# Moving ScalarE and VectorE work inside the second attention of a two-block network: layer-norm silu in two parts, row operands ahead of slab roundings and exponentials

## The reference, cut to what matters

```python
def mixer_ab(h, w_in, conv_w, ln_g, ln_b, w_out):
    u = h @ w_in
    u_val, u_gate, q, k, v = jnp.split(u, ...)
    z = causal_depthwise_conv(u_val * sigmoid(u_gate), conv_w)     # 31 taps, 512 channels
    ya = jax.nn.silu(layernorm(z, ln_g, ln_b))
    yb = moba_attention(q, k, v)                                   # 8 heads of 64, ALiBi, causal at 256 tokens
    return jnp.concatenate([ya, yb], axis=-1) @ w_out
```

## Time and profile before

| what | value |
| --- | --- |
| median of three runs | 894.98 us (894.68 to 895.58) |
| the profiled execution | 894.98 us, span 893.2 us, mean granted clock 0.995 |
| PE busy | 871.1 us, 98% of the span |
| DVE, ACT, POOL busy | 606.9, 470.1, 94.0 us |
| second attention with its projection rows | about 356 to 440 us |
| `mixer_c` up to its projection's end | about 630 to 703 us |

### The profile page before, as it was taken

One profiled execution on the slowest core, in us unless ns is written; L12 is line 12 of the kernel. 1 busy time (PEld: TensorE's weight loads), 2 busy tenths in 40 slices (PEclk: granted clock), 3 DMA queues, 4 the chain that ended last, 5 costly groups with the idle time before them and its releaser, 6 DMA issues.

```text
span 893.2 us, 19362 instructions
## 1 busy us (share of the span) xinstructions
PE 871.1 (98%) x7310; PEld 839.0 (94%) x7310; DVE 606.9 (68%) x994; ACT 470.1 (53%) x755; POOL 94.0 (11%) x139
## 2 busy tenths in 40 slices
PE   8999999999999999997999999999999999999996
PEld 8988899999999999776899999999899999999996
DVE  4766568656656688786766666667979976666665
ACT  6546766434434485356654444445777644444443
POOL 3320002000000039410110000001210100000000
PEclk9999999999999999998999999999999999999999
DMA  7533346565565558422555555555435565555551
GB/s 248 169 120 99 111 138 219 189 207 178 176 203 180 182 167 236 150 96 95 165 189 188 188 188 188 188 189 189 142 123 172 171 204 186 190 189 190 187 180 48
DMA packets 44434, 152.10 MB, mean 170 GB/s; under 512 B 5604, under 2 KB 6884, under 8 KB 44388
## 3 DMA queue, kind: packets, MB, share of 16 engines
q1 hardware_dynamic: 41184, 145.52, 49.7%
q0 software_dynamic: 2400, 4.89, 1.8%
q10 hardware_dynamic: 804, 1.04, 0.3%
HBM read 148.64 MB, written 1.05 MB: 168 GB/s over the span
## 4 chain that ended last, share of the span: by engine, by line
PE 89%; DVE 5%; ACT 4%; issue 1%; DMA 1%; SPq 0%; DVEq 0%; ACTq 0%
PE bank L1342 27%; PE bank L1344 26%; PE bank L1343 26%; DVE alo L938 2%; PE bank L1692 1%; DVE wlo L914 1%; PE bank L1376 1%; PE bank L1426 1%; ACT whi L509 1%; PE bank L1471 1%; DMA raw<-in_slabs 1%; PE bank L1448 1%; PE bank L1370 1%; DVE af L1302 1%; DVE h L948 1%
## 5 line engine op out<-in xcount | busy, mean ns | idle before, releaser
L1342 PE MATMUL bank<-ahi,whi 128*128 128x256 f32 (+1 forms) x1400 | 401.3, 287 | 6.9 <-DVE alo L932 6.1
L1343 PE MATMUL bank<-alo,whi 128*128 128x256 f32 (+1 forms) x1400 | 394.7, 282 | 0.0
L1344 PE MATMUL bank<-ahi,wlo 128*128 128x256 f32 (+1 forms) x1400 | 394.6, 282 | 0.0
L914 DVE TENSOR_TENSOR wlo<-raw,whi 128x1024 fp32r<-128x1024 f32 x273 | 332.7, 1226 | 31.1 <-ACT whi L509 31.0
L509 ACT ACTIVATE whi<-raw 128x1024 fp32r<-128x1024 f32 x273 | 282.7, 1051 | 103.3 <-PE bank L1344 93.4
L1342 PEld LDWEIGHTS bank<-ahi,whi 128*128 128x128 f32 x1400 | 264.8, 189 | 11.1 <-DVE alo L932 6.7
L1343 PEld LDWEIGHTS bank<-alo,whi 128*128 128x128 f32 x1400 | 264.8, 189 | 0.4
L1344 PEld LDWEIGHTS bank<-ahi,wlo 128*128 128x128 f32 x1400 | 265.0, 189 | 0.0
L1342 PE MATMUL bank<-hidhi,whi 128*128 128x256 f32 x704 | 195.0, 277 | 0.5 <-issue 0.5
L1344 PE MATMUL bank<-hidhi,wlo 128*128 128x256 f32 x704 | 195.1, 277 | 0.0
L1343 PE MATMUL bank<-hidlo,whi 128*128 128x256 f32 x704 | 194.4, 276 | 0.0
(11 more groups left out here) (222 smaller groups left out, 721.3 us busy)
## 6 DMA issues: line engine op xcount, KB each, us to landing
raw<-in_slabs SPq DMA_DIRECT2D x273, 512.0 KB, 3.4
shared<-in_convw POOLq DMA_DIRECT2D x4, 512.0 KB, 6.7
shared<-zpad POOLq DMA_DIRECT2D x48, 35.5 KB, 3.5
raw<-in_slabs SPq DMA_DIRECT2D x8, 128.0 KB, 5.6
vtok<-in_gatew POOLq DMA_DIRECT2D x2, 512.0 KB, 4.1
out<-y SPq DMA_DIRECT2D x4, 256.0 KB, 2.7
h<-in_xT ACTq DMA_DIRECT2D x3, 272.0 KB, 5.4
h<-in_xT SPq DMA_DIRECT2D x1, 272.0 KB, 3.6
```

The costliest lines, as they stand in the source:

```text
L914: dve.tensor_tensor(wlo[:, n % R, :, :], raw[:, n % R, :, :], whi[:, n % R, :, :].bitcast(F32), ALU.subtract).then_inc(lo_done, 1)
L1342: pe.matmul(dst, hi, xh, start=start, stop=False, skip_group_check=True)
L1343: pe.matmul(dst, hi, xl, start=False, stop=False, skip_group_check=True)
L1344: return pe.matmul(dst, lo, xh, start=False, stop=stop, skip_group_check=True)
```

## The change

- In the second attention ACT's order changes. In even slots the roundings of slabs (`split_ahead`) come after the transposed probabilities, the pair's output copy and the exponentials; odd slots up to 11 keep theirs in front. Row operands come before the roundings. Operand 0 is made at the end of slot 11 rather than at the start of 12. Output copies go ahead of the exponentials (`PAIR_STEP`), the fourth behind the loop. The exp/tanh table is still loaded in slot 13, but tanh and scaled copy of chunks 0, 1 run in slot 15 and of 2, 3 in slot 17 (were all four in slot 13, ahead of operand 1).
- DVE: the layer norm's product moves from slot 13 to 12, the join of silu follows ACT to slots 15 and 17, slab rests go to the places in `DVE_SPLITS`, the first two final residuals from slot 11 to 18, and behind the loop the three last operands are made ahead of rests and residuals.
- ACT rounds the last three slabs behind operand 7 and around the table load for exp/ln.
- First attention: DVE makes the projection's operand 0 before a slab's rest (`ROW1_SLOT - 1`).
- `mixer_c`: gate products of chunk k run after column k+3, 6 and 7 together after column 9 (were 0 after 3, 1 and 2 after 4, then one each). ACT rounds operand 0 in column 13 rather than 14; DVE's gated output 0 and operand 0 follow `take` of column 13.

```diff
+PAIR_STEP = {6: 0, 10: 1, 14: 2}
+LN_MEAN_STEP, LN_VAR_STEP, LN_NORM_STEP, SILU_STEP = 9, 11, 13, {15: (0, 1), 17: (2, 3)}
-FINAL_RESIDUAL, RESIDUAL_ROW = {11: (0, 1)}, {5: (2, 3), 6: (4, 5), 7: (6, 7)}
+FINAL_RESIDUAL, RESIDUAL_ROW = {18: (0, 1)}, {5: (2, 3), 6: (4, 5), 7: (6, 7)}
+DVE_SPLITS = {13: (-1,), 14: (0, 1), 16: (2,), 17: (3,), 18: (4,)}
-GATES = {3: (0,), 4: (1, 2)} | {k + 2: (k,) for k in range(3, KC)}
+GATES = {k + 3: (k,) for k in range(6)} | {9: (6, 7)}
...
             for u in range(MOBA_U + 3):                      # ACT
-                if u in IN2_STEP or u in OUT2_STEP:
+                slab = u in IN2_STEP or u in OUT2_STEP
+                if slab and u % 2 and u < max(IN2_STEP) + 1:
                     split_ahead(n)
                     n += 1
...
+                    if u in PAIR_STEP:
+                        pair = PAIR_STEP[u]
+                        act.wait_ge(o_ready, FOX_S + 2 * pair + 2)
+                        act.activation(af[:, PAIR_CHUNK[pair], :], aux_bank[:, 0:SEQ], ACT.Copy).then_inc(af_ready, 1)
...
                         probabilities(u // 2, FOX_S, MOBA_N)
+                if u in CAT2_STEP and u > max(IN2_STEP) + 1:
+                    operand_hi(A_CAT2, F_CAT2, CAT2_STEP[u])
+                if slab and (u % 2 == 0 or u > max(IN2_STEP)):
+                    split_ahead(n)
+                    n += 1
...
+                if u == max(IN2_STEP):
+                    act.wait_ge(slab_used, OUT2)
+                    operand_hi(A_CAT2, F_CAT2, 0)
...
                 if u == LN_NORM_STEP:
                     exp_tanh_tables()
-                    for k in range(CONV_C):
+                if u in SILU_STEP:
+                    for k in SILU_STEP[u]:
                         act.wait_ge(ln_norm, k + 1)
...
             for i in range(max(CAT2_STEP.values()) + 1, KC):
+                if i == KC - 1:
+                    act.wait_ge(o_ready, FOX_S + MOBA_S)
+                    act.activation(af[:, PAIR_CHUNK[3], :], aux_bank[:, 0:SEQ], ACT.Copy).then_inc(af_ready, 1)
                 operand_hi(A_CAT2, F_CAT2, i)
-                split_ahead(OUT2 + i)
+            split_ahead(OUT2 + KC - 3)
+            split_ahead(OUT2 + KC - 2)
             exp_ln_tables()
...
+            split_ahead(OUT2 + KC - 1)
             residual_hi(N_MLP0)
...
-                if i == 14:
-                    operand_hi(A_LRU, F_LRU, 0)
                 if i in (13, 14):
                     gelus(3 * (i - 13), 3 * (i - 12))
+                if i == 13:
+                    operand_hi(A_LRU, F_LRU, 0)
...
-                if u == ROW1_SLOT:                           # DVE, first attention
-                    operand_lo(A_MIX1, 0)
...
+                if u == ROW1_SLOT - 1:
+                    operand_lo(A_MIX1, 0)
                 if u >= 1:
                     split_ahead(n)
...
                 softmax_slot(u, MOBA_S, FOX_S, MOBA_N, alibi_bias)   # DVE, second attention
-                if u == LN_NORM_STEP:
+                if u in CAT2_STEP and u > max(IN2_STEP) + 1:
+                    operand_lo(A_CAT2, CAT2_STEP[u])
+                if u == LN_NORM_STEP - 1:
                     dve.wait_ge(ln_std, 1)
...
-                    take(n, acc_bank[n % 2], c, QSCALE if 8 <= c < 12 else 1.0, ahead=n < OUT2 - 1)
+                    take(n, acc_bank[n % 2], c, QSCALE if 8 <= c < 12 else 1.0, ahead=u < 8)
                     n += 1
+                    if u > 8 and n < OUT2:
+                        split_ahead(n - 1)
+                if u == 9:
+                    split_ahead(n - 1)
...
+                if u >= max(IN2_STEP) + 2:
+                    for m in DVE_SPLITS.get(u, ()):
+                        split_ahead(OUT2 + m)
...
             for i in range(max(CAT2_STEP.values()) + 1, KC):
                 operand_lo(A_CAT2, i)
+            for i in range(max(CAT2_STEP.values()) + 1, KC):
                 split_ahead(OUT2 + i)
                 for k in RESIDUAL_ROW[i]:
                     final_residual(k)
...
-                if i >= 14:                                  # DVE, mixer_c
-                    gated_output(i - 14)
-                take(IN3 + i, col_bank(i), c, ahead=IN3 + i < OUT3 - 1 and i not in (10, 14))
-                if i == 14:
+                if i == 15:
+                    gated_output(1)
+                take(IN3 + i, col_bank(i), c, ahead=IN3 + i < OUT3 - 1 and i != 10)
+                if i == 13:
+                    gated_output(0)
                     operand_lo(A_LRU, 0)
-                    split_ahead(IN3 + i)
```

More of the change, by code:

```diff
@@ L118 @@
 OUT2_ORDER = (4, 5, 6, 0, 1, 2, 3, 7)
-LN_MEAN_STEP, LN_VAR_STEP, LN_NORM_STEP, SILU_STEP = 9, 11, 13, 15
+PAIR_STEP = {6: 0, 10: 1, 14: 2}
+LN_MEAN_STEP, LN_VAR_STEP, LN_NORM_STEP, SILU_STEP = 9, 11, 13, {15: (0, 1), 17: (2, 3)}
 PLAIN_COLUMN = 4
-FINAL_RESIDUAL, RESIDUAL_ROW = {11: (0, 1)}, {5: (2, 3), 6: (4, 5), 7: (6, 7)}
+FINAL_RESIDUAL, RESIDUAL_ROW = {18: (0, 1)}, {5: (2, 3), 6: (4, 5), 7: (6, 7)}
+DVE_SPLITS = {13: (-1,), 14: (0, 1), 16: (2,), 17: (3,), 18: (4,)}
 SQUARES_ROWS, SQUARES_CHUNKS = {1: (0,), 3: (2,), 7: (4, 6)}, {1: (0,), 3: (2,), 5: (4,), 7: (6,)}
-GATES = {3: (0,), 4: (1, 2)} | {k + 2: (k,) for k in range(3, KC)}
+GATES = {k + 3: (k,) for k in range(6)} | {9: (6, 7)}
 IN3_ORDER = tuple(range(8, 16)) + tuple(range(8))
@@ L757, in _ @@
             for u in range(MOBA_U + 3):
-                if u in IN2_STEP or u in OUT2_STEP:
+                slab = u in IN2_STEP or u in OUT2_STEP
+                if slab and u % 2 and u < max(IN2_STEP) + 1:
                     split_ahead(n)
                     n += 1
-                if u == max(IN2_STEP) + 1:
-                    act.wait_ge(slab_used, OUT2)
-                    operand_hi(A_CAT2, F_CAT2, CAT2_STEP[u])
                 if u % 2 == 0:
@@ L797, in _ @@
                                        bias=half_gb[:, CONV_C + k:CONV_C + k + 1]).then_inc(ln_half, 1)
-                if u in CAT2_STEP and u > max(IN2_STEP) + 1:
-                    operand_hi(A_CAT2, F_CAT2, CAT2_STEP[u])
             for i in range(max(CAT2_STEP.values()) + 1, KC):
+                if i == KC - 1:
+                    act.wait_ge(o_ready, FOX_S + MOBA_S)
+                    act.activation(af[:, PAIR_CHUNK[3], :], aux_bank[:, 0:SEQ], ACT.Copy).then_inc(af_ready, 1)
                 operand_hi(A_CAT2, F_CAT2, i)
-                split_ahead(OUT2 + i)
+            split_ahead(OUT2 + KC - 3)
+            split_ahead(OUT2 + KC - 2)
             exp_ln_tables()
@@ L1182, in _ @@
                     operand_lo(A_CAT2, CAT2_STEP[u])
-                    split_ahead(OUT2 - 1)
                 softmax_slot(u, MOBA_S, FOX_S, MOBA_N, alibi_bias)
-                if u == LN_NORM_STEP:
+                if u in CAT2_STEP and u > max(IN2_STEP) + 1:
+                    operand_lo(A_CAT2, CAT2_STEP[u])
+                if u == LN_NORM_STEP - 1:
                     dve.wait_ge(ln_std, 1)
@@ L1190, in _ @@
                     c = IN2_STEP[u]
-                    take(n, acc_bank[n % 2], c, QSCALE if 8 <= c < 12 else 1.0, ahead=n < OUT2 - 1)
+                    take(n, acc_bank[n % 2], c, QSCALE if 8 <= c < 12 else 1.0, ahead=u < 8)
                     n += 1
+                    if u > 8 and n < OUT2:
+                        split_ahead(n - 1)
+                if u == 9:
+                    split_ahead(n - 1)
                 if u in OUT2_STEP:
-                    split_ahead(n)
                     n += 1
-                if u in CAT2_STEP and u > max(IN2_STEP) + 1:
-                    operand_lo(A_CAT2, CAT2_STEP[u])
+                if u >= max(IN2_STEP) + 2:
+                    for m in DVE_SPLITS.get(u, ()):
+                        split_ahead(OUT2 + m)
                 if u < len(TAPS_SLOT):
                     tap = taps(tap, TAPS_SLOT[u])
-                if u == SILU_STEP:
+                if u in SILU_STEP:
                     dve.wait_ge(af_ready, KC * F_CAT2 + 3)
-                    for k in range(CONV_C):
+                    for k in SILU_STEP[u]:
                         dve.wait_ge(ln_half, k + 1)
```

## The result

The changed kernel takes 885.82 us (median of 4 runs, 885.51 to 886.07); the kernel before took 895.10 beside it (4 runs, 894.68 to 895.58): a ratio of 0.9892, 95% interval 0.9880 to 0.9904. That is 9.3 us less, where 9.9 less and 885.1 us were forecast.

A forecast was written before the change was run, and what follows sets the result against it. PE was taken to bound the kernel, busy 871.1 of 893.2 us, so only its waits and clock could be won. 0.6 + 6.9 + 1.4 + 1.0 = 9.9 us off 894.98 gave 885.1 us, range 883.0 to 888.3.

The forecast's parts named there:

- Slots 0 to 13: Second attention: PE's waits of 0.4, 1.1 and 0.6 shrink, so PE reaches slot 14 1.7 us earlier.
- Row 1 and the clock: Second projection, slot 14: row 1 starts without a wait and with full clock, ending 8.5 us earlier.
- The new gap: Transposes after slot 15's values: PE waits 1.6 us for DVE's normalizing, queued behind a slab rest awaiting ACT's rounding.
- the rival with the clock: Clock falls while PE is quiet 1.6 us before row 2, costing 1.6 us more: 886.7 us; 22%.
- the slower one: Clock falls before row 2 and stays lower through rows 2 to 7: 13.9 us more, 899.0 us; 3%.
- The tail: End of second projection: 0.7 us wait before row 5, row 7 starts 6.9 earlier, boundary behind it 1.4 shorter.
- First attention: Operand 0 made before the slab rest removes PE's 0.63 us wait at the first projection's first row: 0.6 us.
- mixer_c: Later gate products start column 10 1.45 us earlier; operand 1 of the last projection comes 1.0 us earlier.
- the rival that it slows down: In mixer_c DVE's taps slow beside GpSimd's products, so the 1.0 us gain is lost: 886.1 us; 15%.
- The boundary did not stay: Rival behind the second projection: DVE's residuals or GpSimd's sums set the boundary, no 1.4 us gain: 886.5 us; 10%.
- the wait did not only move: Rival, slots 13 to 16: late roundings make PE wait as long for a `wlo`: about 894.5 us; 3%.
- first three rivals: Clock falls before row 2 (22%), VectorE keeps its mixer_c pace (15%), boundary stays (10%); two together give 888.3 us.

The follow-up runs named there:

- silu in two parts alone: Kernel before with only tanh and scaled copy split over slots 15 and 17 and the fourth output copy moved behind the loop; 891.39 us.
- silu whole: Changed kernel with all eight tanh and copies back in slot 13, but behind operand 1; 891.61 us.
- the longer gap: Changed kernel with the first two final residuals moved from slot 18 to slot 14, ahead of normalizing; median 886.79 us.

## Why the prediction was right, point by point

- **Slots 0 to 13.** Forecast 1.7 us by slot 14, from three waits of which 0.4 would remain. Measured 408.14 against 410.06, 1.9, of which 0.2 was there from the start; the wait that remains is 0.47.
- **Row 1 and the clock.** Forecast 8.5 us by the end of row 1; measured 411.99 against 420.76, 8.8 with the same 0.2 in it. The experiment with silu in two parts alone shows that the eight activations made the large gap.
- **The new gap.** Forecast 1.6 us at the transposes of slot 16, from DVE held in slot 14 by ACT's rounding; measured 1.67, in the same place, and one rest moved by one slot removes it. In the traced run the clock held: neither the rival with the clock nor the slower one came true there.
- **The tail.** Forecast a wait of 0.7 before row 5; measured 0.77. The whole part to the next column came to 8.35 less the 0.17 at 142 us, 8.2, where 8.3 was the sum of 6.9 and 1.4. Its two terms each missed by a little and nearly cancel: row 7 starts 7.24 earlier (437.69 - 430.45), 7.1 without the 0.17, and the boundary gives 1.1 (11.86 to 10.75) and not 1.4. That the moved table load gave it is read from the chain and not from a run that undoes it alone: before, ACT went without a pause from a rounding through the load to its first operand at 440.68, for which PE waited 0.50; now the load runs beside row 6 and ACT waits 0.38 for `h` (first operand at 432.35). The Trainium skill ("ScalarE: Activation LUTs", section "What ACT_TABLE_LOAD costs") has about 2.66 us for a table switch, and by it, as an estimate, ACT's last rounding would have ended at 433.3 and run into the boundary. The changed trace doesn't agree: ACT works again 1.30 us after the load's start (429.03 to 430.33).
- **First attention: wrong.** The failed step is "DVE's later work moves by 0.1, under 1 us of slack". It looked at DVE only. Row 1's operand hung on ACT's three activations, of which the first waits for DVE's masking. Before, PE came to row 1 just as its operand was done (`alo` 109.51 to 109.93, row 1 from 110.02), so an earlier row 0 met the same operand. Worth 0 instead of 0.6 in the run that undoes it.
- **mixer_c: mechanism right, size too large.** Column 10 came 1.5 earlier, as forecast (1.45). From there the sum had operand 1 at 1.0 earlier; it was 0.66 (9.01 - 8.35). DVE's pace was as forecast (takes at 640.14, 643.46, 646.76 and 650.20, 3.3 to 3.4 apart), so the rival that it slows down did not come true. But DVE was 0.4 late at `take` 13 (665.57 + 8.35 against 673.55), and ACT's list from the exponentials' table load on was 1.25 us earlier (654.34 + 8.35 against 663.94), not the 1.6 of the forecast. That operand 0's new place takes time was in the working (DVE's list "holds rest, gelu wait and operand 0 in a row"), but counted as part of one number and not against the old place, which is 0.5 us better.
- **The other rivals.** The boundary did not stay (10.75 for 11.86), and the wait did not only move: in slots 13 to 18 PE waits for no `wlo`. In the forecast's chances one sum is off: two of the first three rivals together make 887.5 to 888.1 us, not 888.3.

Sum: 0.2 of the start, 0 + 8.2 + 0.6 make 8.9 to 9.0 us, which is the trace's 8.9; forecast 9.9. The start's 0.2 is no part of the change. The medians differ by 9.3, within the spread of the runs. The two parts that failed or fell short account for the 1.0 us by which the trace misses the forecast (0.6 and 0.34); that the medians come nearer (9.3 against 9.9) is chance.

## What to carry to other kernels

When a wait goes, look for the next one on the same chain: the operand after it, on the other engine that makes it. A part that the medians cannot separate may be worth nothing or cost time, so each part deserves its own run with only that part undone: here one of the parts was worth 0 and one cost 0.5 us, in a change that won 9. Work that is not due soon, or that waits for another engine, belongs behind whatever in its own queue PE needs next; two such moves gave 2.2 us.

## What was not expected of the hardware

After the end of PE's work the granted clock fell at 1.8 us in the kernel before (gap of 5.00) and at 1.3 us with silu whole (gap of 3.39), where PE had also stood idle for 0.76 just before its last 0.44 us of work. It did not fall within gaps of 1.57 and 1.67 us, nor within the one of 2.46 us in the profiled run with the longer gap. So a gap's length alone did not tell in these traces whether the clock falls.

Nor did one trace tell for all runs of a kernel. Five kernels have the new gap of 1.7 us, the changed one and four of the experiments. Of their 21 runs three (887.66, 886.92, 889.28) are 1.6 to 1.9 us above the median of the same kernel's other runs, and of the four with the 2.46 us gap two (887.45, 889.40) are 1.5 and 3.5 above the other two. The mean granted clock of these five is 0.996 or 0.997 where most of the others have 0.998 or 0.999; the three kernels in which one rest is moved, which have no such gap, have no such run in twelve. The rival "the clock falls in the new gap" priced its fall at 1.6 us, so it may have come true in single runs. That is not shown: none of the five was traced, and 0.997 stands beside some short runs too.
